# The first expert's rows picked on chip by one-hot products instead of a gather, in a one-core decoder step with a mixture of experts

## What is computed

```python
h = rmsnorm(x, W['norm_ffn_w'])
glog = t @ w_rg                                # 4 groups, top 1
elog = (t @ w_re) of the chosen group          # 4 experts, top 2
act = silu(hg) * hu * gates                    # 16 experts, FF = 512
x = x + einsum('nef,efd->nd', act, w_down)
gate = sigmoid(rmsnorm(x, W['norm_ple_w']) @ w_ple_gate)
x = x + gate * (p @ w_ple_proj)
y = rmsnorm(x, W['final_norm_w'])
```

## Time and profile before

| | us |
|---|---|
| median of 3 runs | 652.38 (649.36, 652.38, 654.05) |
| span of the profiled execution, first to last instruction | 645.5 |
| the median less this span | 6.9 |
| PE busy in the span | 597.3 (93%) |
| DVE, ACT, POOL busy | 292.0, 175.6, 80.8 |
| chain that ended last: PE, DMA, DVE | 71%, 20%, 4% of the span |

### The profile page before, as it was taken

How to read it: one execution, slowest core, us unless ns; L and a number is a source line. 1 busy time by engine, 2 the same in 40 slices (tenths; PEclk the granted TensorE clock), 3 DMA queues, 4 the chain that set the end, 5 groups by cost and what they waited for, 6 DMA issues and landing times.

```text
span 645.5 us, 9639 instructions
## 1 busy us (share of the span) xinstructions
PE 597.3 (93%) x3802; PEld 392.3 (61%) x3802; DVE 292.0 (45%) x943; ACT 175.6 (27%) x421; POOL 80.8 (13%) x101
## 2 busy tenths in 40 slices
PE   4999999999998999999999699999988887999996
PEld 2788888788587887788786333333332332334684
DVE  2388459568559999454211731100110101116574
ACT  3122427621543433636101411111110100100333
POOL 4200023321011112110000021121111101000000
PEclk9999999999999999999999889999998987989999
DMA  9833354999332776728998599999999999998001
GB/s 262 290 131 131 130 201 143 362 332 334 137 102 72 255 225 204 260 96 306 367 393 355 210 415 382 425 425 427 423 425 424 424 422 421 427 410 319 2 1 67
DMA packets 45705, 179.69 MB, mean 278 GB/s; under 512 B 3932, under 2 KB 12576, under 8 KB 37201
## 3 DMA queue, kind: packets, MB, share of 16 engines
q1 hardware_dynamic: 35136, 147.21, 58.4%
q0 software_dynamic: 10000, 30.67, 14.8%
q10 hardware_dynamic: 520, 1.15, 0.5%
HBM read 167.65 MB, written 17.39 MB: 287 GB/s over the span
## 4 chain that ended last, share of the span: by engine, by line
PE 71%; DMA 20%; DVE 4%; ACT 2%; issue 2%; SPq 1%; DVEq 0%; ACTq 0%
PE bank L919 26%; DMA arena<-in_w_exp_up 15%; PE bank L1380 12%; PE bank L1173 9%; PE bank L1418 6%; DMA arena<-in_w_in 5%; PE bank L1516 4%; DVE arena L1843 1%; PE bank L1391 1%; PE bank L1016 1%; PE bank L1131 1%; PE bank L1077 1%; PE bank L1471 1%; PE bank L950 1%; PE bank L1194 1%
## 5 line engine op out<-in xcount | busy, mean ns | idle before, releaser
L919 PE MATMUL bank<-hT,arena 128*128 128x264 f32 x768 | 175.3, 387 | 1.5 <-DMA arena<-in_w_in 1.5
L919 PEld LDWEIGHTS bank<-hT,arena 128*128 128x128 f32 x768 | 144.4, 190 | 27.4 <-issue 2.3
L1380 PE MATMUL bank<-arena,hT 128*64 128x512 f32 x512 | 123.5, 632 | 15.7 <-DMA arena<-in_w_exp_up 10.5
L1380 PEld LDWEIGHTS bank<-arena,hT 128*64 128x64 f32 x512 | 39.5, 145 | 91.0 <-issue 89.3
L1851 DVE SCALAR_TENSOR_TENSOR hT<-hT,sq,bank 128x256 f32<-128x256 f32 x16 | 7.7, 480 | 137.3 <-ACT hT L1766 137.3
L1843 DVE TENSOR_TENSOR arena<-arena 128x256 f32<-128x256 f32 (+7 forms) x146 | 60.4, 458 | 16.3 <-ACT arena L1658 9.9
L1418 PE MATMUL bank<-arena,sq 128*64 128x512 f32 x256 | 58.5, 598 | 0.9 <-ACT sq L1771 0.9
L1173 PE MATMUL bank<-arena 128*128 128x264 f32 x256 | 58.1, 387 | 1.3 <-issue 1.3
L1173 PEld LDWEIGHTS bank<-arena 128*128 128x128 f32 x256 | 48.3, 190 | 10.4 <-issue 2.3
L1766 ACT ACTIVATE hT<-bank 128x256 f32<-128x256 f32 x16 | 6.1, 383 | 141.8 <-PE bank L1380 141.8
L1588 ACT ACTIVATE arena<-bank 128x264 f32<-128x264 f32 x40 | 15.5, 389 | 105.3 <-PE bank L919 105.3
(11 more groups left out here) (313 smaller groups left out, 643.4 us busy)
## 6 DMA issues: line engine op xcount, KB each, us to landing
arena<-in_w_exp_down SPq DMA_DIRECT2D x16, 2048.0 KB, 19.4
arena<-in_w_exp_gate SPq DMA_DIRECT2D x15, 2048.0 KB, 22.5
arena<-in_w_exp_up SPq DMA_DIRECT2D x15, 2048.0 KB, 27.4
arena<-in_w_in SPq DMA_DIRECT2D x13, 2048.0 KB, 11.8
out<-arena POOLq DMA_DIRECT2D x18, 512.0 KB, 6.4
arena<-in_w_out SPq DMA_DIRECT2D x4, 2048.0 KB, 9.8
arena<-in_state_ssm POOLq DMA_DIRECT2D x8, 512.0 KB, 8.7
arena<-in_state_hgrn POOLq DMA_DIRECT2D x8, 512.0 KB, 4.8
```

What stands on the lines that cost most here:

```text
L919: last = mm(ps[:, 0:T], w[:, k, j * P:(j + 1) * P], x, start=(k == 0), stop=(k == KT - 1))
L1380: last = mm(bank[p][r, :].rearrange("p (w f) -> p w f", w=2), xgT[:, p, k % 4, CAP * (k // 4):CAP * (k // 4) + CAP], gu[:, :, k, FF // 2 * ...
```

## The change

The rows of expert 0 are no longer gathered. DVE makes a float32 one-hot `hot` of expert 0 (128 x 3 x 64), and PE multiplies `htok` with it (`first_rows`), which gives the turned rows in `bank[2]` directly: 8 tiles of the model dimension x 3 token tiles. `first_at` and the early gather now serve expert 1. `keep_busy` is gone. `table(0)` moves into the middle of `halves_gate_up(0)`, and on DVE the twelve one-hots of the other experts move ahead of what is made from `table(0)`.

The sums of squares are made with the squares as the stationary operand and one column of ones (`token_sums`), so that they come out with tokens on the partitions; ACT takes two small roots (`token_roots`). The last tile's squares are no longer added on DVE but summed by a second round of products. `weighted(c)` follows its own tile at once. Router parts 4 and 5 move ahead of `mix(7)`. The same form is used for the last norm. SP loads expert 2's down weights when `hrow_out` is reached, and `ple_weights` waits for `first_rows`.

```diff
+SUMS_1 = KT - 2
+SUMS_2 = SUMS_1 + KT - 1
+SUMS_3 = SUMS_2 + KT - 2
...
+        hot = hT_all[:, 1024:1024 + 3 * CAP].rearrange("p (t s) -> p t s", t=3)
...
             eng.wait_ge(hrow_out, 48)
-            eng.wait_ge(main.rows[0], 16)
             load_down(2)
+            eng.wait_ge(main.x_full, 1)
             ple_weights(ld_pp)
...
-                at = row_of[:, 0, t:t + 1] if t else first_at[:, 0:1]
+                if t == 2:
+                    eng.wait_ge(tab_ready, 1)
+                at = row_of[:, 0, t:t + 1] if t > 1 else first_at[:, 0:1]
...
-            gather_halves(0)
-            eng.wait_ge(tab_ready, 1)
             move_tokens(1, CHECK + 3)
...
+            def token_sums(ps, x, first):
+                for i, (t0, n) in enumerate(TOK):
+                    last = mm(ps[0:n, i:i + 1], x[:, t0:t0 + n], ones[:, 0:1], start=(first and i == 0),
+                              stop=(not first and i == 2), skip_group_check=True)
+                return last
...
-                if c >= 6:
-                    for k in ((0, 1, 2, 3) if c == 6 else (4, 5)):
+                if c == 6:
+                    for k in range(6):
                         router_part(k)
+            ps = open_a("norm", 1)
+            eng.wait_ge(sq_sum, SUMS_1)
+            token_sums(ps, sq[:, 0], True)
             for c in range(6, KT):
                 router_part(c)
-            norm_sum(1, sq[:, 0])
+            eng.wait_ge(sq_done, 2 * KT)
+            token_sums(ps, sq[:, KT - 1], False).then_inc(a_full, 1)
...
+            def first_rows(ks):
+                for k in ks:
+                    h, j = k // 4, k % 4
+                    for i, (t0, n) in enumerate(TOK):
+                        x = htok[0:n, i, HALF * h:HALF * h + HALF].rearrange("p (q j) -> p j q", j=4)[:, j]
+                        last = mm(bank[2][:, j * P + CAP * h:j * P + CAP * h + CAP], x, hot[0:n, i], start=(i == 0),
+                                  stop=(i == 2))
+                return last
+
+            eng.wait_ge(hot_ready, 1)
+            eng.wait_ge(a_took, ja["ht", 2, 1] + 1)
+            first_rows(range(3))
             ps = open_v("idx")
...
-                        last = mm(ps[r, 0:1], OH[:, 0, i], places[:, i, c:c + 1], start=(i == 0 and c == 0),
+                        last = mm(ps[r, 0:1], OH[:, 1, i], places[:, i, c:c + 1], start=(i == 0 and c == 0),
                                   stop=(i == 2 and c == 2))
             last.then_inc(v_full, 1)
+            first_rows(range(3, KT)).then_inc(main.x_full, 1)
...
-            keep_busy(bank[4 + jv["tab", 0] % 4], 3)
-            eng.wait_ge(rv_ready, 1)
-            table(0, 0, TAB0)
...
                     if t == 0 and k == 3:
                         last.then_inc(gu_half, 1)
+                        eng.wait_ge(rv_ready, 1)
+                        table(0, 0, TAB0)
...
-            eng.wait_ge(a_took, ja["ht", 2, 1] + 1)
-            halves_rows(0)
...
+            def token_roots(k, ps, done):
+                activation(rtok[:, k, 0:2], ps[:, 0:2], ACT.Sqrt, scale=1.0 / D, bias=eps).then_inc(root_ready, 1)
+                activation(rtok[0:NS, k, 2:3], ps[0:NS, 2:3], ACT.Sqrt, scale=1.0 / D, bias=eps[0:NS]).then_inc(done, 1)
...
-                if c:
-                    weighted(c - 1, "mix", R_FFN)
-                if c >= 2:
-                    add_square(c - 1)
-            weighted(KT - 1, "mix", R_FFN)
-            add_square(KT - 1)
+                weighted(c, "mix", R_FFN)
+                if 1 <= c < KT - 1:
+                    add_square(c)
...
+            tt(hot, K[:, K_IOTA:K_IOTA + CAP].rearrange("p (o s) -> p o s", o=1).to_broadcast([P, 3, CAP]),
+               slot1[:, :, 0:1].to_broadcast([P, 3, CAP]), ALU.is_equal).then_inc(hot_ready, 1)
+            one_hots(1, 2)
             one_hots(0, 1)
...
+            one_hots(TAB0, E)
             tables(full("tab", 0), TAB0, 0).then_inc(v_took, 1)
             took("tab", 0)
             row_numbers(TAB0, 0, dve).then_inc(tab_ready, 1)
-            one_hots(TAB0, E)
```

More of the change, by code:

```diff
@@ L226, in make_jobs @@
         v.add("pg", c)
-    a.add("norm", 3)
     v.add("sd")
@@ L1220, in h_row @@
                 last.then_inc(a_full, 1)
-            for half in range(2):
-                h_row(0, half)
+            h_row(0, 0)
             ps = open_v("rt")
@@ L1226, in _ @@
             for i, (t0, n) in enumerate(TOK):
-                nc.tensor.transpose(ps[0:n, 20 * i:20 * i + 20], rstd[0:20, 0, t0:t0 + n], ident[0:20, 0:20])
-            eng.wait_ge(a_took, ja["norm", 1] + 1)
-            turn_factors(ps, 60).then_inc(v_full, 1)
+                last = nc.tensor.transpose(ps[0:n, 20 * i:20 * i + 20], rstd[0:20, 0, t0:t0 + n], ident[0:20, 0:20])
+            last.then_inc(v_full, 1)
+            h_row(0, 1)
             for i in range(1, 3):
@@ L1262, in table @@
                 for t in range(first, turns):
-                    eng.wait_ge(oh_ready, t + 1)
+                    eng.wait_ge(oh_ready, 2 if t == 0 else 1 if t == 1 else t + 1)
                     for i in range(3):
@@ L1388, in halves_rows @@
                 p = t % 2
-                eng.wait_ge(main.rows[p], t // 2 * 16 + 16)
+                eng.wait_ge(main.rows[p], (t // 2 + p) * 16)
                 for j in range(4):
@@ L1518, in _ @@
                 if c == 1:
+                    ps = open_a("norm", 2)
                     eng.wait_ge(sum_took, 3 * KT)
-                    norm_sum(2, sq_end[:, 0])
+                    eng.wait_ge(sq_sum, SUMS_2)
+                    mm(ps[:, 0:T], ones, sq_end[:, 0], start=True, stop=True).then_inc(a_full, 1)
             def out_row(ps, i, half):
@@ L1526, in out_row @@
                 return last
-            out_row(open_a("out", 0, 0), 0, 0)
+            out_row(open_a("out", 0, 0), 0, 0).then_inc(a_full, 1)
+            factors = open_v("sd")
             out_row(open_v("out", 1, 0), 1, 0)
             out_row(open_a("out", 2, 0), 2, 0)
-            norm_sum(3, sq_end[:, 0], 2)
-            ps = open_v("sd")
-            eng.wait_ge(a_took, ja["norm", 3] + 1)
-            turn_factors(ps, 0).then_inc(v_full, 2)
+            eng.wait_ge(sq_sum, SUMS_3)
+            token_sums(factors, sq_end[:, 0], True)
+            eng.wait_ge(sq_done, 4 * KT)
+            token_sums(factors, sq_end[:, KT - 1], False).then_inc(v_full, 2)
             out_row(open_a("out", 0, 1), 0, 1).then_inc(a_full, 2)
@@ L1720, in _ @@
                 square(c, v_took, jv["mix", c] + 1)
-            root(1)
+            token_roots(0, full("norm", 1), a_took)
             def turned_rows(m, t, p):
@@ L1811, in _ @@
             activation(chips[:, 1:2], eps, ACT.Sqrt)
-            root(3)
+            eng.wait_ge(v_full, jv["sd"] + 1)
+            token_roots(1, bank[4 + jv["sd"] % 4], v_took)
             eng.wait_ge(rtok_ready, 3)
-            eng.wait_ge(v_took, jv["sd"] + 1)
             for i in (0, 2):
+                if i == 2:
+                    eng.wait_ge(rtok_ready, 4)
                 t0, n = TOK[i]
@@ L1865, in weighted, with token_factors @@
                 ts(hT[:, c], xT[:, c], col(row + c), ALU.mult).then_inc(norm_done, 1)
-            def token_factors(k, ps):
-                nc.vector.reciprocal(rtok[0:NS, k, 2:3], ps[0:NS, 2:3]).then_inc(rtok_ready, 1)
-                return nc.vector.reciprocal(rtok[:, k, 0:2], ps[:, 0:2])
+            def token_factors(k, sem_, count):
+                eng.wait_ge(root_ready, k + 1)
+                nc.vector.reciprocal(rtok[:, k, 0:2], rtok[:, k, 0:2]).then_inc(rtok_ready, 1)
+                eng.wait_ge(sem_, count)
+                nc.vector.reciprocal(rtok[0:NS, k, 2:3], rtok[0:NS, k, 2:3]).then_inc(rtok_ready, 1)
             nc.vector.memset(chips[:, 1:2], 1.0).then_inc(table_in, 1)
@@ L2241, in _ @@
             ps = full("rt")
-            token_factors(0, ps[:, 60:63]).then_inc(rtok_ready, 1)
+            token_factors(0, a_took, ja["norm", 1] + 1)
             eng.wait_ge(rtok_ready, 2)
@@ L2501, in _ @@
                 add_ple(c)
-            token_factors(1, full("sd")).then_inc(v_took, 1)
-            took("sd")
+            token_factors(1, v_took, jv["sd"] + 1)
+            eng.wait_ge(rtok_ready, 3)
             for half in range(2):
```

25 lines of the change are left out of this document (5 added, 20 removed).

## The result

The changed kernel took 659.46 us (median of 4 runs, 653.65 to 661.97) against 650.87 for the kernel before (4 runs, 648.68 to 654.05): a ratio of 1.0108, 95% interval 1.0064 to 1.0151. It is 1.1% slower, where 0.3% faster was forecast, and 659.46 lies above the range. The profiled execution, the fastest of the four, took 653.65, with a span of 651.9.

A forecast was written before the change was run, and what follows sets the result against it. A PE chain up to the second expert, DMA bytes after it, then a chain at the end. Gains of 0.9 (second expert's end) and 0.8 (last norm) make 1.7 us: 652.4 - 1.7 = 650.7 us, range 646.5 to 656.5.

The forecast's parts named there:

- Part 2: Picks of the first expert's rows: 48 records at 0.118, 5.7 us (3.8 to 7.9), rows copied by 369.75 against 371.23.
- Part 3: PE's clock: one half-clock stretch falls on the picks, costing 1.56 us; first expert starts at 371.3 and runs at 7.09.
- The row of 3.78 for 32: Profile row pricing the picks: 32 records with 128 x 128 weights in 3.78 us, 0.118 each.
- The upper bound of 7.9: Longest time allowed for the picks, at 0.165 us a record from a short group of four taking 0.66.
- Rival (a): Picks stay at half clock, 5.7 us more instead of 1.56, and the first expert starts low; 656.4 us, chance 0.13.
- Part 1: Way to the routing, with moved router parts and small roots: factors first used at 357.0, 0.3 us earlier.
- Parts 4 and 5: Second expert's end at 388.5, 0.9 us earlier, passed on by the full DMA queue; last norm's end 0.8 less.
- the hidden work: Gates at 371 or 372.5, wanted by `table(0)` at about 374.9; the later one-hots' delay on DVE also stays covered.
- Rival (d): The DMA queue carries SP's earlier load, some 5.7 us, through to the end; 645.9 us, chance 0.06.
- The 6.9 between median and span: Profile's span of 645.5 us lies 6.9 below the median; the change was taken to touch nothing there.

The follow-up runs named there:

- e11: Changed kernel with each load's columns side by side, filler matmuls ahead of the counts and one 512-column filler behind each model tile; one run, 662.06 us.
- e5: Changed kernel with token rows stored by model tile, so that a load's 128 columns lie side by side instead of four apart; ratio to before 1.0135.
- e7: Changed kernel with filler ahead of the counts and 128 instead of 64 columns streaming per pick, load columns still four apart; ratio to before 1.0153.
- e9: Changed kernel with the one-hot stationary and token rows streaming 512 columns wide, a copy and four transposes, no filler; ratio to before 1.0026.
- e3: Changed kernel with three 512-column filler matmuls in PE's idle time ahead of the counting matmuls; ratio to before 1.0104.
- e6: Changed kernel with each load's 128 columns side by side and three filler matmuls ahead of the counts; ratio to before 1.0093.
- e10: Changed kernel with load columns side by side, 128 columns streaming per pick and filler ahead of the counts; one run, 660.1 us.
- e8: Changed kernel with one-hot stationary, token rows streaming 512 wide, copy and four transposes, filler ahead of the counts, later clearing of `xg`; ratio to before 0.9939.
- e12: Kernel before with the moved sums, filler ahead of the counts and later clearing of the gather buffer, keeping the gather; ratio to before 1.0025.
- e4: Changed kernel with the 24 pick products ordered by token tile, the 8-row ones last, instead of by model tile; ratio to before 1.0090.

## Why the prediction was wrong

**Parts 2 and 3 failed together: what a record costs, and the clock.** Part 2's step was "48 x 0.118 = 5.7", which is 0.71 for the six records of a model tile. Part 3's step was "I expect one such stretch to fall on the picks, at the same price", 1.56, with the first expert at 7.09 behind it. That took it for granted that PE earns the clock back on the picks, as it had on `keep_busy`. It did not: 0.50 through all the picks and 3 us of the first expert. The six records took (14.9 - 0.65) / 8 = 1.78.

Two things make them so long, and each does it nearly alone. Side by side and at full clock the six take 0.92 (e11's first group), with the switches between full and 8-row loads in it, for which Part 2 had nothing. At half clock they take 1.66 side by side ((13.9 - 0.65) / 8, e5). With columns four apart they take 1.79 at full clock (e7, with products twice as wide). So mending only the clock would have left the picks at about 8 x 1.79 = 14.3 (an estimate from e7's one group), and mending only the columns left 13.25 (e5). With both mended, and fillers in between, the same 48 took 6.9 (e11). The loss can't be divided between the two by adding.

The row of 3.78 for 32 had full loads only, with columns side by side, at a granted 1.00, and was no neighbour for loads that alternate, whose columns lie apart, at half clock. The upper bound of 7.9, from a group of four, held none of these. That 8-row loads are not free was right. On the first expert the low clock alone cost 1.3: with `table(0)` it took 8.96 for 7.64.

Rival (a), at a chance of 0.13, had the low clock right, 0.50 as the picks end. Its price of 5.7 came near the 7.2 that the picks took beyond the forecast, but in part by luck: it priced neither the step nor the switches, and without the low clock these records would have been nearly as long. Its reason was right and the skill's only in part. The Trainium skill's page "TensorE: Matmul & The Clock Gate", section "HAM oscillation — how this bites in real kernels", puts such losses down to idle gaps between bursts. The trace agrees in e9, where the clock is low behind 2.98 of idle time, but e3, e6, e7 and e10 lose it within the picks with PE recorded as busy; e11 keeps it over the same gap as e6, and e8 over the same 0.69 as e3.

**Part 1: small, but the wrong sign.** Relative to the last tile's addition, the factors are used 3.62 later, against 4.18 before (357.28 - 353.10); with the 0.98 for the moved router parts that is 0.4 later, not 0.3 earlier. The step counted the path through ACT's table. Its roots are done at 357.44 (357.20 + 0.24), but the last wait is for the turned logits: `weighted(7)`, the last router part, DVE's copy of the logits, their transposes. `weighted(7)` took 0.70 instead of 0.35, as POOL cleared `xg` at the same time; in e8, with the clearing later, it took 0.36 and the factors came 3.28 after the addition.

**Parts 4 and 5 were right, and the hidden work stayed hidden.** From the first expert's end to the second's it was 388.65 to 398.22, 9.57, as 1.11 + 1.37 + 7.09 gave. The gates came at 375.3, later than the 372.5 of the forecast, because `idx` stood behind 5.4 of picks, but `table(0)`, at 384.64 after longer picks, did not wait for them, and the later one-hots delayed nobody. At the forecast's 374.9 the gates would have been 0.4 late; the longer picks moved both. The queue was dry before expert 4's load, so the delay passed on: of the 8.8 between the two profiles (398.22 and 389.45), 7.1 are left at the last norm's sum (644.50 and 637.41). Rival (d) is out. At the end, the last sum to the output took 645.79 - 644.50 = 1.29, 0.6 less than the 1.93, within 0.3 to 1.2.

**The sum.** The second expert's end was forecast at 388.5 and came at 398.2: the picks started 1.2 later (1.1 of that at the factors' first use, 0.4 of it from a mixer that was itself later in this execution), were 7.2 longer than forecast with the low clock, and the first expert 1.3 longer: 9.7. Relative to the mixer, A is 7.36 longer; with the 0.98 ahead of it and 0.6 gained at the end that makes 7.7, and the runs give 0.0108 x 650.87 = 7.0 (4.2 to 9.8). The 6.9 between median and span that the prediction took over was mostly not start and end: time less span is 1.8 here (653.65 and 651.9), so the execution profiled before was some 5 quicker than its median.

What stays open: which property of the picks lets the clock fall. Idle time just ahead is ruled out as the only cause (e8 and e11 keep the clock over the waits of e3 and e6), 64 columns as the only cause (e7, e10); that the clock stays with dense products in between is shown, in one execution (e11). The picks spend most of their time in weight loads (7.74 of 9.00 busy in the stretch above, where the first expert has 1.98 of 5.50), but this share wasn't varied by itself. Nor is it shown why a step of four columns costs the picks so much: the transposes of `xg` read with the same step, and four of them took 0.75 in e8.

## What to carry to other kernels

Price a new burst of matmuls by rows with the same shape of load, the same step between its columns and the same granted clock, and ask whether the burst itself keeps the clock up: these picks, mostly weight loads, did not, and what followed began at half clock too. Selecting rows by a one-hot is better done with the one-hot as the small stationary operand and the rows streaming 512 columns wide (12 records in 2.94 at full and 5.58 at half clock, against 48 in 14.25 at half clock); with the copy and the transposes that it then needs it is 4.5 and 7.5 against 14.9. Filler paid only where PE did not idle long between it and the work that it was meant for (0.69 in e8, 2.72 in e12).

## What the runs showed of the hardware

- Six float32 records with a 128-column load each, four on 128 rows and two on 8: 0.92 side by side at full clock (e11's first group), 1.66 side by side at half clock (e5), 1.78 with columns four apart at half clock (the changed kernel), 1.79 with columns four apart and products of 128 columns at full clock (e7).
- Alternating 128-row and 8-row loads cost 2.5 over 24 products, nearly all of it at half clock (e4).
- The clock fell in a stretch in which PE was recorded as busy throughout (e6, 371.27 to 375, behind a wait of 1.76), and stayed up over a wait of 1.74 with dense products between the same picks (e11).
- A DVE operation from SBUF to SBUF took 0.70 instead of 0.35 while POOL cleared a buffer. The Trainium skill's page "SBUF — State Buffer", section "SBUF: two separate sides", says that some DVE operations and POOL's share a pair of ports which one holds for a whole instruction; the trace agrees with it (0.36 in e8, where the clearing came later). In the kernel before, DVE's operation came ahead of POOL's second clearing and kept its 0.35, and the two clearings took 1.14 instead of 0.98.
